# The end of the first mixer with constant matrices and pairs of tiles, and one activation table for logarithm and exponential in ten layer norms

## What is computed

```python
def _layer_norm(x, g, b):
    mu = jnp.mean(xf, -1, keepdims=True)
    var = jnp.mean(jnp.square(xf - mu), -1, keepdims=True)
    return (xf - mu) * lax.rsqrt(var + LN_EPS) * g + b
...
# first_block, for each of two layers
    m = mixer(x * (1 + sc1) + sh1)
    x = _layer_norm(ALPHA * x + (1 + ga1) * m, ...)
    y = (silu(u @ w_gate) * (u @ w_up)) @ w_down
    x = _layer_norm(ALPHA * x + (1 + ga2) * y, ...)
...
# the end of _rwkv7_mixer: y is the state's output, (tokens, head, 64)
    mean = jnp.mean(y, -1, keepdims=True)
    var = jnp.mean(jnp.square(y - mean), -1, keepdims=True)
    y = ((y - mean) * lax.rsqrt(var + RWKV_GN_EPS)).reshape(B, T, D) * gn_g + gn_b
    bonus = jnp.sum(r * k * r_k, -1, keepdims=True) * v
    return ((y + bonus) * g) @ w_out
```

## Time and profile before

| | us |
|---|---|
| median of 3 runs | 2289.92 |
| lowest, highest | 2289.46, 2291.46 |
| profiled execution | 2288.5 |
| its span, first to last instruction | 2286.5 |

### The profile page before, as it was taken

The page is one execution under the profiler, slowest core; times in us unless marked ns, Lnnn a source line. Parts: engine busy times, 40 slices in busy tenths (PEclk is TensorE's granted clock), DMA queues, the critical chain, the costliest instruction groups (busy, mean ns, idle before and its releaser), DMA issues.

```text
span 2286.5 us, 40831 instructions
## 1 busy us (share of the span) xinstructions
PE 2107.3 (92%) x17730; PEld 1913.5 (84%) x17730; DVE 1189.3 (52%) x2188; ACT 903.0 (39%) x1297; POOL 709.1 (31%) x316
## 2 busy tenths in 40 slices
PE   4988987999989988999999898899999998989997
PEld 3867766889889887898999895699989997858897
DVE  6165444764582446662642566464255427547652
ACT  0442122454354224554433453443343334434543
POOL 0350001314674003127314560131451166304124
PEclk9999998999999989999999998899999999989999
DMA  8563441455434003555444440244534453304552
GB/s 328 227 275 149 150 150 74 148 186 190 155 133 148 2 2 129 185 187 182 148 177 173 147 148 19 92 166 167 181 135 181 168 181 114 129 20 147 188 193 81
DMA packets 49682, 340.44 MB, mean 149 GB/s; under 512 B 6368, under 2 KB 8416, under 8 KB 8672
## 3 DMA queue, kind: packets, MB, share of 16 engines
q1 hardware_dynamic: 49504, 337.84, 40.7%
HBM read 336.77 MB, written 1.05 MB: 148 GB/s over the span
## 4 chain that ended last, share of the span: by engine, by line
PE 81%; DVE 10%; ACT 4%; issue 2%; DMA 1%; POOL 1%; SPq 0%; ACTq 0%; DVEq 0%; POOLq 0%
PE bank L532 80%; DMA ada_ring<-ada 1%; POOL ring_low L2503 1%; DVE arena L1931 1%; DVE arena L1903 1%; ACT L1451 1%; PE bank L538 1%; ACT high L1477 1%; DVE arena_parts L1926 1%; DVE acc L1993 1%; DVE arena L1890 1%; DVE ZZ L2110 0%; DVE arena L1918 0%; ACT small L1451 0%; ACT small L1449 0%
## 5 line engine op out<-in xcount | busy, mean ns | idle before, releaser
L532 PE MATMUL bank<-arena_parts,high 128*128 128x272 f32 (+2 forms) x4512 | 1024.8, 315 | 58.5 <-ACT arena_parts L1502 36.8
L532 PEld LDWEIGHTS bank<-arena_parts,high 128*128 128x128 f32 x4512 | 748.9, 191 | 108.4 <-issue 47.3
L532 PE MATMUL bank<-arena_parts,ring_low 128*128 128x272 f32 (+2 forms) x2736 | 781.6, 288 | 0.0
L1477 ACT ACTIVATE high<-ring 128x2048 fp32r<-128x2048 f32 x237 | 453.0, 1914 | 670.5 <-PE bank L532 592.9
L2503 POOL TENSOR_TENSOR ring_low<-ring,high 128x2048 fp32r<-128x2048 f32 x105 | 485.3, 4627 | 679.5 <-ACT high L1477 679.5
L532 PEld LDWEIGHTS bank<-arena_parts,ring_low 128*128 128x128 f32 (+1 forms) x2736 | 523.3, 191 | 1.0
L1939 DVE TENSOR_TENSOR ring_low<-ring,high 128x2048 fp32r<-128x2048 f32 x132 | 304.1, 2304 | 180.1 <-ACT high L1477 180.1
L532 PE MATMUL bank<-hidden_high,high 128*128 128x256 f32 (+1 forms) x1056 | 303.2, 287 | 0.0
L532 PE MATMUL bank<-hidden_low,high 128*128 128x256 f32 (+1 forms) x1056 | 301.1, 285 | 0.0
L532 PE MATMUL bank<-hidden_high,ring_low 128*128 128x256 f32 (+1 forms) x1056 | 300.1, 284 | 0.0
L2503 POOL TENSOR_TENSOR hidden_low<-arena,hidden_high 128x256 fp32r<-128x256 f32 (+1 forms) x132 | 111.8, 849 | 574.9 <-DVE hidden_high L1955 574.9
(11 more groups left out here) (310 smaller groups left out, 2285.8 us busy)
## 6 DMA issues: line engine op xcount, KB each, us to landing
ring<-stream SPq DMA_DIRECT2D x269, 1024.0 KB, 4.8
ada_ring<-ada SPq DMA_DIRECT2D x48, 1024.0 KB, 5.5
con<-consts SPq DMA_DIRECT2D x1, 1542.5 KB, 10.7
con<-consts SPq DMA_DIRECT2D x1, 1040.0 KB, 7.0
arena<-xin SPq DMA_DIRECT2D x1, 1024.0 KB, 11.9
out<-arena SPq DMA_DIRECT2D x2, 512.0 KB, 2.9
prob_even<-consts SPq DMA_DIRECT2D x1, 320.0 KB, 11.0
par<-params SPq DMA_DIRECT2D x1, 272.5 KB, 9.7
```

The source lines that it names most:

```text
L532: ins = nc.tensor.matmul(o, l, r, start=start, stop=stop_, skip_group_check=True)
L1477: act(high[:, q % HIGHS], ring[:, s % RING], ACT.Copy).then_inc(a.sig(high_ready), 1)
```

## The change

- **Head norm by constant matrices.** `less_head_mean`, a 128x128 constant (identity less 1/64 inside each head's block of 64), takes the mean away in one matmul per tile (`less_mean`); `HEAD_MEAN` (identity less that constant, made once by DVE into `PP[:, 0]`) gives the mean of the squares, already spread (`variance`). `row_sums` and `spread` of the means and of the inverse roots go, and with them the 16-row steps.
- **Pairs of tiles.** ACT squares from the bank in four instructions of 512 columns, and takes logarithm and exponential of full 512-column pairs (bias 64e-5 from `cols[:, 60:61]`); DVE works pair by pair, and the out projection waits for pairs (`in_pairs`) and no longer for all.
- **The bonus** is spread (`bonus_spread`, 2 pairs each) behind the state matmuls of chunks 1 and 2, and multiplied by DVE before the sums of L2162. Gain, bias and gate are applied in two sets of 8 instructions.
- **`stream_slab` of piece 11**: its four calls stand together behind the variances.
- **Tables.** `preload_act_table_set("natural_log_exp_and_others")` stands in place of the one-element logarithm in `norm`, and once in the first mixer's end. Logarithm and exponential are both in that set.
- **High parts.** `first_highs(0)` ahead of the first norm becomes `norm(SEQ, next_highs(0))`.
- **POOL** waits for piece 11, and no longer for piece 10, ahead of `base_sums`.

```diff
+    add("less_head_mean", (r == c) - (r // 64 == c // 64) / 64.0)
...
+            def less_mean(q):
+                eng.wait_ge(v2p, pe.nth(v2p))
+                for e in range(2):
+                    m = mm(bank[q][:, SEQ * e:SEQ * e + SEQ], mask64("less_head_mean", P), tl(5, 2 * q + e), True, True, hold=e)
+                m.then_inc(told(q, "scalar"), 1)
...
+            def variance(q):
+                b = 4 + q % 2
+                eng.wait_ge(head_squared, pe.nth(head_squared))
+                eng.wait_ge(*freed(b))
+                for e in range(2):
+                    m = mm(bank[b][:, SEQ * e:SEQ * e + SEQ], HEAD_MEAN, tl(3, 2 * q + e), True, True, hold=e)
...
+                bonus_spread(2 * c - 2, (4, 7)[c - 1])
+                bonus_spread(2 * c - 1, (5, 3)[c - 1])
...
+            for q in range(4):
+                less_mean(q)
+            variance(0)
+            variance(1)
             sum_rows(len(PIECES) - 2)
-            eng.wait_ge(v2p, pe.nth(v2p, 4))
-            row_sums(5, 4, "scalar", "hsel", 16)
-            stream_slab(PIECE_SLABS * (len(PIECES) - 1))
-            stream_slab(PIECE_SLABS * (len(PIECES) - 1) + 1)
-            eng.wait_ge(a2p, pe.nth(a2p))
-            spread(small[:, 0, 0:SEQ], "hselT", P, B4, told)
-            eng.wait_ge(a2p, pe.nth(a2p))
-            row_sums(3, 5, "vector", "hsel", 16)
-            stream_slab(PIECE_SLABS * (len(PIECES) - 1) + 2)
-            stream_slab(PIECE_SLABS * (len(PIECES) - 1) + 3)
+            variance(2)
+            variance(3)
+            for q in range(PIECE_SLABS):
+                stream_slab(PIECE_SLABS * (len(PIECES) - 1) + q)
             sum_rows(len(PIECES) - 1)
-            eng.wait_ge(a2p, pe.nth(a2p))
-            spread(small[:, 2, 0:SEQ], "hselT", P, B4)
-            spread(small[:, 1, 0:SEQ], "hselT", P, B4)
-            eng.wait_ge(v2p, pe.nth(v2p))
             eng.wait_ge(late_loaded, 16)
...
             def norm(T, highs=()):
-                act(cols[0:1, 61:62], one[0:1, :], ACT.Ln).then_inc(a.sig(astep), 1)
+                na.preload_act_table_set("natural_log_exp_and_others")
...
+            for q in range(4):
+                eng.wait_ge(full_for_scalar[q], a.nth(full_for_scalar[q]))
+                act(heads(q), in_bank(q), ACT.Square).then_inc(a.sig(head_squared), 1)
+            for q in range(4):
+                b = 4 + q % 2
+                eng.wait_ge(full_for_scalar[b], a.nth(full_for_scalar[b]))
+                act(heads(q), in_bank(b), ACT.Ln, bias=cols[:, 60:61]).then_inc(a.sig(free["scalar"][b]), 1)
+                eng.wait_ge(*a.last)
+                act(heads(q), heads(q), ACT.Exp, scale=-0.5).then_inc(a.sig(head_scaled), 1)
             piece_rows(len(PIECES) - 1)
-            first_highs(0)
-            norm(SEQ), norm_out(0, SEQ)
+            norm(SEQ, next_highs(0)), norm_out(0, SEQ)
...
+            gate = lambda j: tl(US, j, SEQ, META)
+            for j in range(DT):
+                nv.scalar_tensor_tensor(out=tl(8, j), in0=tl(8, j), scalar=pc("gn_b", j), in1=gate(j), op0=ALU.add, op1=ALU.mult)
             for q in range(4):
+                eng.wait_ge(head_squared, v.nth(head_squared))
+                    nv.scalar_tensor_tensor(out=tl(5, j), in0=bank[q][...], scalar=pc("gn_g", j), in1=gate(j), op0=ALU.mult, op1=ALU.mult)
+            for q in range(5):
+                if q < 4:
+                    eng.wait_ge(head_scaled, v.nth(head_scaled))
+                    nv.tensor_tensor(two(5, q), two(5, q), two(3, q), ALU.mult)
+                if q:
+                    nv.tensor_tensor(two(5, q - 1), two(5, q - 1), two(8, q - 1), ALU.add).then_inc(v.sig(v2p), 1)
+                if q == 1:
+                    modulation(len(PIECES) - 2, 7)
             modulation(len(PIECES) - 1, 7)
...
-            eng.wait_ge(piece_summed, len(PIECES) - 1)
+            eng.wait_ge(piece_summed, len(PIECES))
             base_sums(SEQ)
```

More of the change, by code:

```diff
@@ L675, in out_projection @@
                             early_mean(T)
+                        if n == 0 and k % 2 == 0 and in_pairs is not None:
+                            eng.wait_ge(in_pairs, pe.nth(in_pairs))
                         m = mm(bank[b][:, 0:T], w((name, layer, n, k)), rhs(k), k == 0, k == k_tiles - 1,
@@ L2158, in _ @@
                 nv.tensor_tensor(arena[:, (3, 4, 6)[c], :, 0:64], H(c), wl(c), ALU.mult).then_inc(v.sig(state_ready), 1)
+            for q, b in ((0, 4), (1, 5), (2, 7), (3, 3)):
+                eng.wait_ge(full_for_vector[b], v.nth(full_for_vector[b]))
+                nv.tensor_tensor(two(8, q), two(8, q), pair(b), ALU.mult).then_inc(v.sig(free["vector"][b]), 1)
             for j in range(DT):
@@ L2162, in _ @@
                 nv.tensor_tensor(tl(5, j)[:, 64:256], tl(5, j)[:, 64:256], bank[b][:, 64:256], ALU.add).then_inc(v.sig(v2p), 1)
-            eng.wait_ge(*v.last)
-            modulation(len(PIECES) - 2, 7)
-            eng.wait_ge(v2p, v.sent[v2p])
-            for q in range(4):
-                eng.wait_ge(full_for_vector[q], v.nth(full_for_vector[q]))
-                nv.tensor_tensor(two(5, q), two(5, q), pair(q), ALU.subtract).then_inc(v.sig(v2a), 1)
-            eng.wait_ge(full_for_vector[5], v.nth(full_for_vector[5]))
@@ L2170, in _ @@
-            nv.tensor_scalar(small[0:16, 2, 0:SEQ], bank[5][0:16, 0:SEQ], 1.0 / 64, 64e-5, ALU.mult, ALU.add).then_inc(v.sig(v2a), 1)
-            modulation(len(PIECES) - 1, 7)
-            for q in range(4):
-                eng.wait_ge(full_for_vector[q], v.nth(full_for_vector[q]))
-                nv.tensor_tensor(two(5, q), two(5, q), pair(q), ALU.mult).then_inc(v.sig(free["vector"][q]), 1)
-            eng.wait_ge(*v.last)
-            for j in range(DT):
-                nv.tensor_scalar(tl(5, j), tl(5, j), pc("gn_g", j), pc("gn_b", j), ALU.mult, ALU.add).then_inc(v.sig(vstep), 1)
@@ L2178, in _ @@
-            for q in range(4):
-                eng.wait_ge(full_for_vector[q], v.nth(full_for_vector[q]))
-                nv.tensor_tensor(two(3, q), two(8, q), pair(q), ALU.mult).then_inc(v.sig(free["vector"][q]), 1)
-            eng.wait_ge(*v.last)
-            nv.tensor_tensor(S(5), S(5), S(3), ALU.add).then_inc(v.sig(vstep), 1)
-            eng.wait_ge(*v.last)
-            nv.tensor_tensor(S(5), S(5), arena[:, US, :, META:TALL], ALU.mult).then_inc(v.sig(v2p), 1)
+            gate = lambda j: tl(US, j, SEQ, META)
@@ new lines, in _ @@
+            eng.wait_ge(free["vector"][3], v.sent[free["vector"][3]])
+            for j in range(DT):
+                nv.scalar_tensor_tensor(out=tl(8, j), in0=tl(8, j), scalar=pc("gn_b", j), in1=gate(j),
+                                        op0=ALU.add, op1=ALU.mult).then_inc(v.sig(vstep), 1)
+            for q in range(4):
+                eng.wait_ge(head_squared, v.nth(head_squared))
+                for e in range(2):
+                    j = 2 * q + e
+                    nv.scalar_tensor_tensor(out=tl(5, j), in0=bank[q][:, SEQ * e:SEQ * e + SEQ], scalar=pc("gn_g", j), in1=gate(j),
+                                            op0=ALU.mult, op1=ALU.mult).then_inc(v.sig(free["vector"][q] if e else vstep), 1)
```

31 lines of the change are left out of this document (23 added, 8 removed).

## The result

| | before | after |
|---|---|---|
| median | 2289.69 | 2267.33 |
| lowest, highest | 2287.03, 2291.46 | 2260.95, 2269.13 |
| runs | 4 | 4 |
| profiled execution, its span | 2288.5, 2286.5 | 2265.64, 2263.6 |

The ratio is 0.989, with a 95% interval from 0.9864 to 0.9916. The direction was right, and so was what bounds each of the changed parts; the size and the width were not.

The account below looks back on a forecast made before the run. PE bounds the kernel (busy 92%, 81% of the chain), so gains come where the chain leaves PE. -20.9 + 1.6 - 12.9 = -32.2 from 2288.5 gives 2256.3, against the median 2257.7; forecast 2257, range 2251 to 2262.5.

Parts of the forecast that it names:

- part 1: First mixer's end, up to the out projection: it starts at 356.0 and not at 376.9, -20.9 us.
- slab 47 as the turn: First mixer's end: slab 47 may load only once slab 44 is used, lands at 352.3, and PE waits 3.1.
- Part 1's clock: Mixer's end and out projection: granted clock as a term of both signs, 1.8 regained or as much as 1 lost.
- the 1.8 as lost: Out projection's first 15 us: 3.6 us at the lower clock level lose 1.8, kept unchanged in the forecast.
- may be lost in the late stream: Late slab stream of the mixer's end: possible further loss to the low clock, +1.
- low stretches in the rows are 3.4 to 3.6 us long: Profile windows before the change: length of low-clock stretches, used against a slower result, which had chance 0.01.
- Part 2: First norm, high parts moved into it: DVE's L1903 waits for POOL's second low part until 36.3, +1.6 us.
- Part 3: Ten norms: the table load between logarithm and exponential goes, -1.29 each, -12.9 us.
- The Trainium skill's 2.66: Table switch in ten norms, load and drain: would give -26.6; as a rival 2243.5, chance 0.01.
- -1.29, ten times: Ten norms: every saved table load counts in full because all ten exponentials are on the chain, -12.9.
- Rival B: Mixer's end and three norms: the clock stays up behind the shorter idles, -1.8 - 4.5, 2251; chance 0.12.
- rival C: Norms: the tables give nothing and only the mixer counts, 2270.6; chance 0.04.

Follow-up runs that it names:

- the pair of kernels: The changed kernel, and the changed kernel with the first feed-forward's two high parts made ahead of the first norm again: ratios 0.989 and 0.9882.
- the second set of runs: The changed kernel again, same file, for a second profile and more runs: median 2265.26 of 6 runs, ratio 0.9891.

## Why the prediction was wrong in size

**What bounds the kernel, and part 1's mechanism: right.** PE's chain through state, bonus, mean, variances and slabs; slab 47 as the turn (the forecast's steps behind it add up to 355.85 and not 355.95, which changes nothing); transfer 4.85 against 4.9; PE's wait 3.24 against 3.1; DVE's last pair, which ended at 354.2, 2.1 ahead of slab 47's landing at 356.3, as forecast (350.2 and 352.3), hidden. At the full clock the price was right to 0.3 us: 32.23 with the wait filled for 32.5, and 29.44 without the wait for 29.5.

**Part 1's clock: the step that failed.** The forecast said "So I keep the 1.8 as lost": it carried the loss that lay in the out projection over as it was, and put what "may be lost in the late stream" at +1, in neither sum nor range. That 1.8 did stay (33.72 for 33.80 to the logarithm). But behind a wait of 3.24 the low level comes first on what follows the wait, slab 47 (+0.9) and the row sum (3.57 for 1.95, +1.6), and these are on the chain: 2.5 us. The other 1.6 is the first set of bonus blocks (3.16 for 1.99) and the state matmuls ahead of it (1.59 for 1.15), priced at the full clock too. Together 4.1; the executed path is 3.9 longer than with the wait filled, and 3.6 longer than the forecast. In the four executions with the wait unfilled the excess over 32.5 was 3.6, 3.7, 1.7 and 1.1; in the last two both bonus sets ran at full clock, and in the last slab 47 too, so that the row sum alone took 3.57. What the wait cost behind itself is thus 1.6 to 2.5, and the forecast's "low stretches in the rows are 3.4 to 3.6 us long" was too short: its window of 377 to 392 cut one off that had begun at 373.9 and lasted 6.8, and the one behind slab 47 lasted 10.2.

**Part 2: right.** POOL's first low part started at 27.0 after the out projection's start (forecast 27.0), the second ended at 36.0 (36.3), L1934 started at 34.6 (34.7) and took 1.2 longer for it (1.6). It eats this norm's table, as the pair of kernels shows.

**Part 3: right in mechanism and unit, short in the total.** 1.25 to 1.30 in each stretch without a mixer, but the last has 0.9 in the changed kernel. That isn't the table: with the tables taken out again this stretch is 196.32, 1.24 above the changed kernel's 195.08, so something else in the changed kernel costs 0.35 there; what, is open. The Trainium skill's 2.66 for a switch ("ScalarE: Activation LUTs", "What ACT_TABLE_LOAD costs") is not borne out: the change takes both the load and the handover away, and 1.28 is what goes. In the stretches with mixers, for which the forecast had 3.9 and the two profiles show 1.0, the clock's part is larger than the table; there the step that failed is the count, "-1.29, ten times", as if nothing between a norm's first tile and the next norm could take it back. Rival B expected 1.5 us where the clock stays up behind the shorter idle. The clock did stay up more: in the stretches of norm 4 to 5, 6 to 7 and 9 to 10 the low level lasted 3.4 us instead of 6.8 (worked out as the length times twice the clock's distance from 1), and they gained 1.26, 1.30 and 0.9, the table and no more. The traces show why the clock brought nothing: in these stages PE's 97th matmul, some 14 us behind its first tile, needs POOL's low part. Norm 9 to 10 in the kernel before and in the changed one:

```profile
2096.99 0.47 PE L532 MATMUL bank<-arena_parts,high 128*128 128x512 f32 x1 [0.59 <-POOL ring_low L2503]
2075.35 0.47 PE L535 MATMUL bank<-arena_parts,high 128*128 128x512 f32 x1 [0.68 <-POOL ring_low L2542]
```

A faster PE ahead of that waits longer there (norm 4 to 5: 0 before, 0.36 in the changed kernel; norm 6 to 7: 0.09 and 0.70), and the low part comes earlier only as far as the norm does. The kernel before alone shows it too: norm 9 to 10 with 6.7 us low took 195.96, with 3.5 us 195.98.

**The sum and its range.** The median lies between the forecast and rival C's 2270.6 (the tables give nothing), but C isn't it: the loads are gone, and each stretch without a mixer is shorter. The sum was made from one profile with every PE-bound stretch at that profile's clock, and the three runs shown lay within 2 us, so the range had no term for it. Starting from the median instead of the profile had already taken in 1.4 of the profile's being short. The 36 runs of the kernel before that stood beside the experiments lay between 2283.09 and 2299.82. A term of about 3 us to each side would have taken the range to 2265.5, still short; with the 3.6 priced in part 1 (a forecast of 2260.6) the median of 2267.33 would lie at 6.7 above, and that of the second set of runs, 2265.26, at 4.7. Of that, 2 to 5 us are the tables' total (8.2 and 10.8 for 12.9), which lies in the stretches with mixers and isn't settled; the rest, up to 5 us, no run here places.

## What to carry to other kernels

When waits are taken out of a chain and one new wait is left, price what stands right behind it at the lower clock level too, not only the wait; here a wait of 3.2 us cost 1.6 to 2.5 more in the 6 us behind it. Moving the consumer of a ring slot ahead of work that doesn't need it (slab 44 before the variances) removed the wait and this cost, 4.2 to 5.1 us; the 1.7 or 1.8 lost in the next stage it did not remove. Ask of a saved piece in each place whether what comes next waits for something else. A profile's long, busy stretches aren't constants: read a second profile before stretches are compared, and compare stretches that repeat when an edit of 1 us is to be seen (those without a mixer repeated to 0.05 us here, with two exceptions of 0.6 and 0.9).

## What was not expected of the hardware

- Useless work on TensorE in a wait paid: 3.29 us of matmuls that nobody reads kept the clock at 1.00, and the path to norm 1's logarithm became 5.7 us shorter. Of these 1.6 are the bonus blocks and state matmuls, which lie ahead of the filled wait and ran at the full clock in that execution anyway, so the filling earned 4.1 at most; against the unfilled execution in which these ran at the full clock too, with the high parts ahead of the norm (67.15), it is 3.0. That is one profiled execution, and the medians and ratios of the whole kernel don't settle it.
- The low level's share varies without any edit: in the mixer's end of the kernel before, in one execution of four, it lasted so long that the end took 55.72 us instead of 53.46 or 53.47; the stretch from the program's start to the first state varied by 8.3 us (321.9 to 330.2).
- DVE's 128x256 instructions with two inputs from SBUF and POOL's low part did not run beside each other: two of them took 1.98 instead of 0.76 while POOL's 4.5 us instruction ended. Some small DVE instructions of 8 columns beside POOL's base sums took 0.58 to 0.70 instead of 0.17.
